# Moving a one-core transformer kernel's SBUF tensors to other addresses, with no instruction changed

## The reference

```python
h = rmsnorm(x, norm_mix_pre)
y_a = gla_mixer(...) @ w_branch_gla; y_b = swa_mixer(...) @ w_branch_swa; y_c = pool_mixer(...) @ w_branch_pool
merged = gate[0] * y_a + gate[1] * y_b + gate[2] * y_c
x = x + rmsnorm(merged @ w_out, norm_mix_post)
x = x + rmsnorm(conv_ffn(rmsnorm(x, norm_ffn_pre), ...), norm_ffn_post)
x = x + fox_mixer(rmsnorm_2(x, fox_norm), ...)            # 16 heads, causal, forget gates
x = x + conv_ffn_2(rmsnorm_2(x, ffn_norm[0]), ...)
k_nope, k_rope, v = mla_shared_kv(x, ...)
x = x + mla_mixer(rmsnorm_2(x, mla_norm), ..., k_nope, k_rope, v, cos, sin)   # 16 heads
x = x + conv_ffn_2(rmsnorm_2(x, ffn_norm[1]), ...)
return rmsnorm_2(x, final_norm)
```

## The kernel before, in words

| tensor | before | after |
|---|---|---|
| `X` | 16.1 to 32.1 | 144.2 to 160.2 |
| `HH`, `HL` (and `MOH`) | 32.1 to 64.1 | 16.1 to 48.1 |
| `RAW` | 64.1 to 80.1 | 160.2 to 176.2 |
| `WHI` | 80.1 to 96.1 | 176.2 to 192.2 |
| `WLO` | 96.1 to 112.1 | 192.2 to 208.2 |
| `PAR`, `CON`, masks, `RSTD`, `SUMSQ`, `SQ` | 112.1 to 127.8 | 208.2 to 223.9 |
| arena | 127.8 to 223.9 | 48.1 to 144.2 |
| `ACTH` | 127.8 to 171.8 | 48.1 to 92.1 |
| `ACTL` | 171.8 to 215.8 | 92.1 to 136.1 |
| `YH` / `YL` | 174.7 to 198.7 / to 222.7 | 95.0 to 119.0 / to 143.0 |
| `MH`, `ML` | 127.8 to 159.8 | 48.1 to 80.1 |
| `FOH` / `FOL` | 179.8 to 195.8 / to 211.8 | 100.1 to 116.1 / to 132.1 |
| `CQH`, `CQL`, `LH`, `LL` | 127.8 to 159.8 | 48.1 to 80.1 |
| `MOL` | 191.8 to 223.8 | 112.1 to 144.1 |

## Time and profile before

### The profile page before, as it was taken

One profiled execution on the slowest core, in us unless ns is written; L12 is line 12 of the kernel. 1 busy time (PEld: TensorE's weight loads), 2 busy tenths in 40 slices (PEclk: granted clock), 3 DMA queues, 4 the chain that ended last, 5 costly groups with the idle time before them and its releaser, 6 DMA issues.

```text
span 2686.7 us, 30214 instructions
## 1 busy us (share of the span) xinstructions
PE 2392.4 (89%) x10784; PEld 1868.6 (70%) x10784; DVE 1050.9 (39%) x1590; ACT 921.8 (34%) x1194; POOL 837.1 (31%) x204
## 2 busy tenths in 40 slices
PE   4997459986999897799899998989999999999897
PEld 3885338874788685766578886866766767788685
DVE  3551233344455502445435554123333321455501
ACT  3223222223544322344444442243232222544321
POOL 2320004432344342322134443342222223344342
PEclk9996569998999998899999999988999999999998
DMA  3110002231222222111022221222111112222221
GB/s 142 65 58 23 0 12 94 94 109 47 78 94 94 74 86 82 64 62 47 32 79 94 94 94 65 96 97 79 47 47 56 53 47 94 78 94 94 74 87 73
DMA packets 30175, 194.68 MB, mean 72 GB/s; under 512 B 3361, under 2 KB 3505, under 8 KB 13617
## 3 DMA queue, kind: packets, MB, share of 16 engines
q1 hardware_dynamic: 30128, 194.06, 20.3%
HBM read 191.95 MB, written 2.10 MB: 72 GB/s over the span
## 4 chain that ended last, share of the span: by engine, by line
PE 86%; DVE 6%; issue 4%; ACT 3%; POOL 1%; DVEq 0%; ACTq 0%; POOLq 0%
PE ps L395 23%; PE ps L396 22%; PE ps L397 22%; PE ps L657 5%; PE ps L680 3%; PE ps L420 1%; PE ps L422 1%; PE ps L421 1%; PE ps L671 1%; PE ps L489 1%; PE ps L428 1%; POOL WLO L385 1%; ACT SP L963 1%; PE ps L548 1%; PE ps L659 1%
## 5 line engine op out<-in xcount | busy, mean ns | idle before, releaser
L385 POOL TENSOR_TENSOR WLO<-RAW,WHI 128x2048 fp32r<-128x2048 f32 (+2 forms) x200 | 836.9, 4185 | 1820.3 <-ACT WHI L827 1820.3
L395 PE MATMUL ps<-HH,WHI 128*128 128x512 f32 x1600 | 640.0, 400 | 14.3 <-DVE HL L1191 9.5
L396 PE MATMUL ps<-HL,WHI 128*128 128x512 f32 x1600 | 629.4, 393 | 0.0
L397 PE MATMUL ps<-HH,WLO 128*128 128x512 f32 x1600 | 628.7, 393 | 0.0
L827 ACT ACTIVATE WHI<-RAW 128x2048 fp32r<-128x2048 f32 (+2 forms) x200 | 344.9, 1725 | 269.5 <-PE ps L397 206.2
L395 PEld LDWEIGHTS ps<-HH,WHI 128*128 128x128 f32 x1600 | 304.6, 190 | 98.1 <-issue 27.1
L396 PEld LDWEIGHTS ps<-HL,WHI 128*128 128x128 f32 x1600 | 304.8, 190 | 65.0 <-issue 2.6
L397 PEld LDWEIGHTS ps<-HH,WLO 128*128 128x128 f32 x1600 | 304.0, 190 | 65.0
L395 PE MATMUL ps<-ACTH,WHI 128*128 128x512 f32 x528 | 212.3, 402 | 27.3 <-DVE ACTL L1449 27.3
L1009 ACT ACTIVATE CV<-U,PAR 128x512 f32<-128x512 f32 x132 | 107.8, 817 | 367.1 <-DVE U L1188 367.1
L396 PE MATMUL ps<-ACTL,WHI 128*128 128x512 f32 x528 | 211.5, 400 | 0.0
(11 more groups left out here) (252 smaller groups left out, 3287.4 us busy)
## 6 DMA issues: line engine op xcount, KB each, us to landing
RAW<-weights SPq DMA_DIRECT2D x127, 1024.0 KB, 4.8
RAW<-weights SPq DMA_DIRECT2D x48, 704.0 KB, 4.0
RAW<-weights SPq DMA_DIRECT2D x24, 768.0 KB, 4.1
X<-xT SPq DMA_DIRECT2D x1, 2048.0 KB, 10.1
outT<-X SPq DMA_DIRECT2D x1, 2048.0 KB, 6.3
RESET<-resets SPq DMA_DIRECT2D x1, 512.0 KB, 10.6
RAW<-weights SPq DMA_DIRECT2D x1, 512.0 KB, 3.6
CS<-rope SPq DMA_DIRECT2D x1, 512.0 KB, 4.2
```

Of the source, the lines that this page charges most:

```text
L385: pool.tensor_tensor(WLO[:, slot, 0:cols], RAW[:, slot, 0:cols], WHI[:, slot, 0:cols].bitcast(F32), ALU.subtract).then_inc(w_lo, 1)
L395: pe.matmul(out, wh, hh, start=first, stop=False)
L396: pe.matmul(out, wh, hl, start=False, stop=False)
L397: return pe.matmul(out, wl, hh, start=False, stop=last)
```

## The change

`HH` and `HL` are allocated first, then 98,336 bytes are set aside for the arena, and `X`, the weight buffers and everything small come above. The tensors that lie over others (`MOH`, `FB` over `HH`/`HL`; `QRS`, `RT` over `SQ`) move with them. Sizes, instructions, semaphores and their order are the same on every engine: five tables of instructions that differ in nothing but line numbers.

```diff
+ARENA = 98336
...
-        keep = Region((nc.sbuf_base + 31) // 32 * 32)
+        low = Region((nc.sbuf_base + 31) // 32 * 32)
+        hh_at = low.at
+        HH = low("HH", [P, KD, T], F32R)
+        HL = low("HL", [P, KD, T], F32R)
+        arena = low.at
+        above = arena + ARENA
+        keep = Region(above)
         X = keep("X", [P, KD, T])
-        hh_at = keep.at
-        HH = keep("HH", [P, KD, T], F32R)
-        HL = keep("HL", [P, KD, T], F32R)
         RAW = keep("RAW", [P, 2, SLOT])
         WHI = keep("WHI", [P, 2, SLOT], F32R)
         WLO = keep("WLO", [P, 2, SLOT], F32R)
...
         RS = keep("RS", [P, 2, NT])
-        arena = keep.at
...
+        assert max(mix.at, tmp.at, small.at, ffn.at, fox.at, mla.at) <= above, ([r.at-arena for r in (mix,tmp,small,ffn,fox,mla)], keep.at)
```

## The result

The changed kernel takes 2696.55 us (median of five runs, 2694.73 to 2703.35); the kernel before, 2687.08 in the same comparison (five runs, 2678.3 to 2687.91). The ratio is 1.0048, 95% interval 1.0034 to 1.0062: slower by half a per cent, where half a per cent faster was forecast, and outside the range. (The ratio amounts to 12.9 us and the medians lie 9.5 apart; the five runs of before spread over 9.6.)

A forecast was written before the change was run, and what follows sets the result against it. TensorE was taken to bound the kernel, at 86% of the chain. Terms of -17.1 and +3.9 summed to -13.2 us, taking 2686.7 to 2673.5; with 0.6 more the forecast was 2674 us, range 2664 to 2690.

The forecast's parts named there:

- What bounds the kernel: Whole program: TensorE's matmuls are 86% of the chain of waits, so a nanosecond per matmul counts in full stretches.
- My reading: a moving operand costs 6.7 ns more above some limit: 512-column fp32r matmuls: 6.7 ns more per start above a limit between 112.1 and 127.8 KiB, taken as 128.
- the count of two slow starts per triple: mlao's high, low, high sequence: one far tile slows its own matmul and the next, mean 231.1 ns.
- 1, the arena's 17.1 us: Arena tiles come down to 48 to 144 KiB; those below 128 KiB turn fast, 17.1 us gained.
- 2, nothing for `HH`/`HL`: `HH`/`HL` move from 32 to 16 KiB, both on the fast side: nothing for their 4800 matmuls.
- 3, groups by token +3.9: `WHI`/`WLO` rise as moving operands: 576 matmuls of 256 columns slow by 6.7 ns, 3.9 us lost.
- 4, stationary operand, taken as nothing: `WHI`/`WLO` rise as stationary operands under 7968 512-column fp32r matmuls: a large unknown, counted as nothing.
- 5, 6, 7: Attention matmuls (up to 4.3 us gain possible), VectorE, ScalarE and GpSimd (+-2 us), and DMA: each taken as nothing.
- The rival "both operands must be low": A far stationary operand also costs 6.7 ns, or both must share a side: 35.9 us slower, 2723; chance 0.18.
- `HH` at 233: Sign in the profile after: matmuls on `HH` at 233 would prove the rival that both operands must be low.
- "Addresses do nothing": Rival: the 6.7 ns belong to the stages through what other engines do; no change, 2687; chance 0.10.
- the prediction's 215.8 ns: Every 512-column matmul's cost by the skill's rule, columns at 2.4 GHz plus 2.5 ns; it would make the sum zero.

The follow-up runs named there:

- the kernel with half the split: Kernel before, but GpSimd subtracts only the first half of each weight chunk's columns in the three up stages: 2675.78 us, ratio 0.9973.
- before with 32 bytes: The kernel before with one edit, its arena starting 32 bytes higher (130,944 in place of 130,912): 2665.38 us, ratio 0.9930.

## Why the prediction was wrong, point by point

- *What bounds the kernel*: right. TensorE's 6.7 ns per matmul is what the time follows; the three kernels with `HH` and all arena streams but `YH`/`YL` at 226.7 gained 0.7 to 0.9%.
- *My reading: a moving operand costs 6.7 ns more above some limit*: this step failed. The rows were right, 226.7 and 233.3, but in the kernel before height and remainder go together: `HH` is low and has the weights' remainder, each arena tile is high and misses it, by 32 (`YH`/`YL` by 96). mlao, which I took for the test, mixes both in the same way, and the count of two slow starts per triple is no rule: the same addresses gave 233.3 in the kernel with half the split. I read a table in KiB where 130,912 bytes stood beside 82,048. The remainders of both layouts could have been worked out before the run.
- *1, the arena's 17.1 us*: nothing came. The arena did get `HH`'s remainder, 128, but the weights had left it for 160 in the same edit. The sum itself was sound: 17.1 against 18.8 to 23.6 by the three ratios, which also have the tiles that I left slow.
- *2, nothing for `HH`/`HL`*: +17.6 us, the largest term of the result, and it came through item 4.
- *3, groups by token +3.9*: -1.3. They too change with the distance, but the 256-column ones are slowest at 0: 120.0, against 117.2 at the 32 of the changed kernel.
- *4, stationary operand, taken as nothing*: as a cost of height that was right; the weights at 192 to 224 KiB cost nothing. What I missed is that it enters as a distance to the moving one. The 128-column rows couldn't show it, being bounded otherwise: 112 ns in every layout.
- *5, 6, 7*: no effect seen. `X` and `CV` keep their VectorE times, and the attention matmuls theirs, apart from the clock.
- *The rival "both operands must be low"* had the direction at 0.18, by a wrong mechanism, and 35.9 us for 9.5: 32.0 became 17.6 (of these 14.4 us, the up stages' wait for weights is 33 passes of 0.36, 11.9 us), 3.9 became -1.3, and the clock gave some 9 back in the profiled execution. The prediction said that `HH` at 233 would prove this rival. It came so, and it proved nothing of the kind: with the weights alone moved up, or `HH` and the weights both high, `HH` is at 226.7.

"Addresses do nothing" was rejected for the right reason, rows in one program that differ. The Trainium skill, *SBUF — State Buffer*, "Who interferes with whom", gives TensorE two SBUF read ports, independent of each other, and says that TensorE never waits on anyone. That gives no reason to expect what is measured here: the time of a matmul depends, by 3%, on how far its moving operand lies from its stationary one. Whether a port waits, no run here shows. The same page, "Operand start alignment", asks for no more than element alignment and says that its runs timed nothing; here 32 bytes are worth 0.7%. On the prediction's 215.8 ns: in the Trainium skill, *TensorE: Matmul & The Clock Gate*, "Back-to-back issue gap" calls that formula the gap of an isolated matmul, and gives about 131 ns for a stream of weight loads and matmuls at 512 columns. The starts here, 226.7 to 234.3, agree with neither.

## What to carry to other kernels

When rows of one program differ by operand, write down the addresses in bytes, with remainders modulo 32 to 256, beside heights and sides; an explanation by region and one by remainder can fit the same rows, and a kernel with another spacer between two tensors costs one run. In a hand-placed SBUF, give the moving and the stationary operands of the long fp32r streams of 512 columns the same remainder modulo 256, and let no small tensor or odd-sized arena stand between them unpadded. And price a faster or slower TensorE only as far as the engine that feeds it: a wait of 0.4 us per pass hid more than half of the loss in the up stages.

## What the runs showed that was not expected

- A 512-column fp32r matmul starts every 226.7 ns when moving and stationary operands are a multiple of 256 bytes apart and 228.9 to 234.3 otherwise. The cause is not settled: a conflict of the two reads in some unit of 32 bytes or more fits, and no run here shows it. Distances between the remainders, below 32 bytes, weren't tried, nor other types of operand.
- In mlao, whose stream mixes two distances, the mean start is not what the two have alone: 231.1 and 233.3 for the same pair 0 and 224, 232.0 for 0 and 64 (alone 226.7 and 228.9), 231.1 for 160 and 128 (alone 234.3 and 232.4). So the table of remainders holds for streams of one distance, and something else enters in a mixed one.
- With 256 columns and swapped roles, alignment is not better: 120.0 aligned and also at 96, 116.7 and 117.2 at 32, 117.8 to 118.7 at 64, 128, 160 and 224.
- At the lower level of the clock the 512-column starts are 427 ns apart whatever the distance, in down0 of before (224) as in that of the kernel with weights and `HH` low (0); the effect is one of the upper level.
- Three layouts tie at the best time: 2662.64 us (weights low), 2663.24 (weights high, aligned), 2665.38 (before with 32 bytes). Their ratios' intervals overlap. The last is one number in one line.
